# An encoder layer's expert stage: tiles of 96 slots of one expert and 32 of another group's, one accumulating scatter each

## The reference, cut to what matters

```python
g_idx = top_k(softmax(h @ w_rg + b_rg), 1)                  # one group of 4
e_idx = top_k(softmax(le of that group), 2)                 # two experts in it
a = einsum('bsd,edf->bsef', h, w_gate)                      # 1024 -> 256 per expert
u = einsum('bsd,edf->bsef', h, w_up)
hid = silu(a) * u * combine[..., None]
x = x + einsum('bsef,efd->bsd', hid, w_down)                # 256 -> 1024
```

## Time and profile before

| | us |
|---|---|
| median of 3 runs | 559.99 (556.28 to 560.72) |
| profiled execution, its own time | 559.87 |
| its span | 558.0 |
| mean granted TensorE clock | 0.930 of full speed |

### The profile page before, as it was taken

The page is one execution under the profiler, slowest core; times in us unless marked ns, Lnnn a source line. Parts: engine busy times, 40 slices in busy tenths (PEclk is TensorE's granted clock), DMA queues, the critical chain, the costliest instruction groups (busy, mean ns, idle before and its releaser), DMA issues. The chain is left out here.

```text
span 558.0 us, 7597 instructions
## 1 busy us (share of the span) xinstructions
PE 499.4 (89%) x2858; PEld 267.9 (48%) x2858; DVE 230.0 (41%) x642; ACT 113.8 (20%) x273; POOL 165.6 (30%) x167
## 2 busy tenths in 40 slices
PE   5898899998998999999999997854999999999970
PEld 3554444444664777665666666553333333333320
DVE  1127444412678834444545555452522322223110
ACT  2200242223232243332222311130011000110010
POOL 1211288850789700000000002221035222222242
PEclk9999799998998999999999977665999999999995
DMA  8999500005100000066000229386589999999712
GB/s 290 427 384 404 231 1 1 1 1 194 50 2 0 1 1 0 2 260 267 1 0 1 75 81 374 150 321 234 169 324 342 400 377 388 378 375 380 226 25 32
DMA packets 29609, 100.04 MB, mean 179 GB/s; under 512 B 5376, under 2 KB 6912, under 8 KB 29184
## 3 DMA queue, kind: packets, MB, share of 16 engines
q1 hardware_dynamic: 21216, 84.03, 39.1%
q0 software_dynamic: 5904, 8.43, 6.3%
q10 hardware_dynamic: 2448, 7.04, 3.3%
HBM read 77.39 MB, written 35.21 MB: 202 GB/s over the span
## 5 line engine op out<-in xcount | busy, mean ns | idle before, releaser
L1217 PE MATMUL bank<-arena 128*128 128x512 f32 (+1 forms) x256 | 114.9, 587 | 5.5 <-DVE arena L826 3.1
L1467 PE MATMUL bank<-arena 128*32 128x512 f32 x832 | 93.1, 599 | 0.0
L1192 PE MATMUL bank<-arena 128*128 128x128 f32 (+1 forms) x412 | 61.9, 287 | 21.0 <-DVE arena L908 4.6
L1217 PEld LDWEIGHTS bank<-arena 128*128 128x128 f32 x256 | 49.6, 196 | 61.4 <-issue 54.7
L1192 PEld LDWEIGHTS bank<-arena 128*128 128x128 f32 (+1 forms) x412 | 50.9, 145 | 57.9 <-issue 44.6
L585 POOL DMA_INDIRECT out<-arena x25 | 38.7, 1549 | 122.6 <-DVE arena L1143 49.6
L1355 PE MATMUL bank<-arena 128*128 128x512 f32 x128 | 65.0, 637 | 0.0
L1467 PEld LDWEIGHTS bank<-arena 128*32 128x32 f32 x832 | 25.8, 111 | 57.9 <-issue 57.9
L908 DVE COPY arena<-bank 128x512 f32<-128x512 f32 (+2 forms) x64 | 36.4, 587 | 36.4 <-PE bank L1192 36.3
L467 POOL TENSOR_SCALAR small<-small 128x1 f32<-128x1 f32 x16 | 3.7, 233 | 157.6 <-ACT arena L680 97.1
L1487 PE MATMUL bank<-arena 128*32 128x512 f32 x416 | 47.0, 592 | 0.8 <-DVE arena L1136 0.8
(11 more groups left out here) (153 smaller groups left out, 517.0 us busy)
## 6 DMA issues: line engine op xcount, KB each, us to landing
arena<-in_w_gu SPq DMA_DIRECT2D x17, 2048.0 KB
arena<-in_w_dn SPq DMA_DIRECT2D x17, 1024.0 KB, 20.6
slot_rows<-arena SPq DMA_DIRECT2D x1, 11308.0 KB, 37.8
arena<-slot_rows ACTq DMA_DIRECT2D x13, 514.0 KB, 6.7
arena<-in_w_out SPq DMA_DIRECT2D x2, 2048.0 KB, 8.0
arena<-in_x SPq DMA_DIRECT2D x4, 512.0 KB, 10.7
arena<-in_w_in_k SPq DMA_DIRECT2D x1, 2048.0 KB, 16.3
arena<-in_w_in_q SPq DMA_DIRECT2D x1, 2048.0 KB, 22.3
```

The lines of the kernel that those rows point to most:

```text
L1192: last = nc.tensor.transpose(TPB[p % 2][0:s.shape[-1], b * P:(b + 1) * P], s, ident)
L1217: last = nc.tensor.matmul(product_bank(i)[:, 0:width], hT[:, k, t * P:(t + 1) * P], w[:, k, :], start=(k == 0), stop=(k == KD - 1))
L1467: last = nc.tensor.matmul(GU[g % 2][BLK * b:BLK * (b + 1), :], xT[g % 2][:, k, BLK * b:BLK * (b + 1)], w_gu[n % RING][:, k, :], start=(k = ...
```

## The change

A tile is now made of two pieces. `TRIPLES` lists, for each group of tiles i, the first three experts of group i and the last expert of group i+2 (modulo 4): [0, 1, 2, 11], [4, 5, 6, 15], [8, 9, 10, 3], [12, 13, 14, 7]. Tile 3i+j holds the 96 slots of the j-th expert and, behind them, slots 32j to 32j+31 of the fourth one. The slots in DRAM stay where they were, so `load_x` needs two DMAs. As the two experts of a tile are of different groups, no token stands in it twice, and one scatter serves the tile; each waits for the one before to land. The weights are loaded in the order `LOADED`, and the table `BUF` says into which buffer each load goes (that whose last tile comes first).

```diff
+TRIPLES = [[EPG * i + j for j in range(3)] + [EPG * ((i + 2) % G) + 3] for i in range(G)]
+LOADED = [TRIPLES[i][j] for i in range(G) for j in (0, 3, 1, 2)]
+def last_tile(n):
+    i, j = divmod(n, 4)
+    return 3 * i + (0, 2, 1, 2)[j] if n < E else ITEMS + n - E
+def buffers():
+    buf, use, before = [], [], []
+    for n in range(E + EXTRA):
+        held = {b: max(m for m in range(n) if buf[m] == b) for b in set(buf)}
+        b = n if n < RING else min(held, key=lambda b: (last_tile(held[b]), held[b]))
...
+            i, j = divmod(g, 3)
+            return 3 * [4 * i + (0, 2, 3)[j]] + [4 * i + 1] if g < ITEMS else 4 * [E + g - ITEMS]
+        def rows_of(g):
+            if g >= ITEMS:
+                return x_dram[g * P:g * P + CAP, :], x_dram[g * P + CAP:(g + 1) * P, :]
+            i, j = divmod(g, 3)
+            own, shared = CAP * TRIPLES[i][j], CAP * TRIPLES[i][3] + BLK * j
+            return x_dram[own:own + CAP, :], x_dram[shared:shared + BLK, :]
+        def adds(g):
+            return 16 * (g // 3 + 1)
...
-            def add(g, run):
+            def add(g):
                 pool.wait_ge(s_ya, g + 1)
                 pool.wait_ge(s_yv, g + 1)
                 pool.wait_ge(s_tag, g + 1)
+                if g > 0:
+                    pool.wait_ge(s_add[(g - 1) % 3], adds(g - 1))
                 nc.gpsimd.indirect_dma_start(
-                    out=out_rows, out_offset=bass.IndirectOffsetOnAxis(ap=tag_row[:, g, run:run + 1], axis=0),
+                    out=out_rows, out_offset=bass.IndirectOffsetOnAxis(ap=tag_row[:, g, 0:1], axis=0),
...
+            for g in range(LAST + 1):
+                add(g)
+                if g < 2:
+                    overflow(2 * g)
+                    overflow(2 * g + 1)
...
-                nc.scalar.dma_start(xg[g % 3], x_dram[g * P:(g + 1) * P, :]).then_inc(s_xg[g % 3], 16)
+                for part, src in ((slice(0, CAP), rows_of(g)[0]), (slice(CAP, P), rows_of(g)[1])):
+                    nc.scalar.dma_start(xg[g % 3][part, :], src).then_inc(s_xg[g % 3], 16)
...
-                nc.vector.tensor_tensor(tag_row[:, g, :], row[:, R_TOK:R_TOK + 1].to_broadcast([P, 2]), cut, ALU.add)
+                nc.vector.tensor_scalar(tag_row[:, g, :], row[:, R_TOK:R_TOK + 1], float(FAR), None, ALU.add)
```

More of the change, by code:

```diff
@@ L49 @@
 RING = 5
+TRIPLES = [[EPG * i + j for j in range(3)] + [EPG * ((i + 2) % G) + 3] for i in range(G)]
[8 more added lines that the diff above has]
+        b = n if n < RING else min(held, key=lambda b: (last_tile(held[b]), held[b]))
+        before.append(held.get(b))
+        buf.append(b)
+        use.append(buf.count(b))
+    return buf, use, before
+BUF, USE, BEFORE = buffers()
 K_TRI, K_ONE, K_E, K_BASE, K_I = 0, P, 2 * P, 2 * P + E, 2 * P + 2 * E
 K_ROW = K_I + EXTRA
-K_CUT = K_ROW + T
-K_MINE = K_CUT + 2 * ITEMS + 1
+K_MINE = K_ROW + T
 NK = K_MINE + ITEMS
@@ L387, in expert @@
                 if n < E:
-                    return n
+                    return LOADED[n]
                 sp.wait_ge(s_extra, 1)
@@ L584, in add @@
                 pool.wait_ge(s_tag, g + 1)
+                if g > 0:
+                    pool.wait_ge(s_add[(g - 1) % 3], adds(g - 1))
                 nc.gpsimd.indirect_dma_start(
-                    out=out_rows, out_offset=bass.IndirectOffsetOnAxis(ap=tag_row[:, g, run:run + 1], axis=0),
+                    out=out_rows, out_offset=bass.IndirectOffsetOnAxis(ap=tag_row[:, g, 0:1], axis=0),
                     in_=y_sb[g % 3], in_offset=None,
                     bounds_check=SEQ - 1, oob_is_err=False, compute_op=ALU.add).then_inc(s_add[g % 3], 16)
[L590 to L613, removed]
+            for g in range(LAST + 1):
[3 more added lines that the diff above has]
+                    overflow(2 * g + 1)
             def extra_pool(g):
-                added(g - 1, 0)
-                add(g, 0)
-                added(g, 0)
+                add(g)
+                pool.wait_ge(s_add[g % 3], adds(g))
             passes(pool, extra_pool)
@@ L1467, in gate_up @@
                         last = nc.tensor.matmul(GU[g % 2][BLK * b:BLK * (b + 1), :], xT[g % 2][:, k, BLK * b:BLK * (b + 1)],
-                                                w_gu[n % RING][:, k, :], start=(k == 0), stop=(k == KD - 1))
+                                                w_gu[BUF[n]][:, k, :], start=(k == 0), stop=(k == KD - 1))
                 last.then_inc(s_gu, 1)
@@ L1488, in down @@
                                                     hidT[g % 2][:, k, BLK * b:BLK * (b + 1)],
-                                                    w_dn[n % RING][:, k, half * 512:(half + 1) * 512],
+                                                    w_dn[BUF[n]][:, k, half * 512:(half + 1) * 512],
                                                     start=(k == 0), stop=(k == 1))
@@ L1557 @@
         np.tile(CAP * p[:E], (P, 1)), np.tile(p[:EXTRA], (P, 1)), p[:, None] + P * p[:T] - FAR,
-        FAR + FAR * np.stack([p[:, None] >= cut, p[:, None] < cut], axis=2).reshape(P, 2 * ITEMS),
-        np.full((P, 1), FAR), (P * p[:ITEMS] + p[:, None]) // CAP], axis=1).astype(f32)
+        *[np.where(p < CAP, t[j], t[3])[:, None] for t in TRIPLES for j in range(3)]], axis=1).astype(f32)
     def by_expert(v, blocks):
```

50 lines of the change are left out of this document (24 added, 26 removed).

## The result

The kernel before took 557.81 us (median of 20 runs, 552.2 to 561.57), the changed one 565.25 us (20 runs, 559.81 to 571.27). The ratio is 1.0135, interval 1.0101 to 1.0168: **slower by 1.35%**, outside the predicted range of 552.4 to 557.8. How long its waits are in the other executions, no trace shows.

What follows compares the result with a forecast made beforehand. PE was taken to bound the expert stage, except at its start and tail. From 559.9 us, -5.0 (tail) and +0.3 (start) sum to -4.7, giving 555.2 us; range 552.4 to 557.8.

Steps and rivals of the forecast that it cites:

- The tail: End of the expert stage: with one scatter for tile 11, the last tile's scatter is issued 5.0 us earlier.
- B: Rival, tail: tile 11's scatter lands within 4.1 us, so the last tile's own data binds; 553.6 us, chance 0.05.
- two loads for a tile's rows: Row loads on ACT: the second DMA costs zero in mid-stage and +0.3 us at the stage's start.
- Weights ... Zero: Weight loads 5 to 16: each issued when it was, tightest slack 4.5 us at tile 10, so zero cost.
- The size of the start: Stage start: the second row piece delays PE's first tile by +0.3 us, bounds 0 to 0.7.
- Rival A: Stage start: the 32-row piece lands only after a further transfer, at most 3 us more; 558.2 us, chance 0.10.
- Rival C: Tile 10: split loads and bunched scatters make weights late; 10 us later would give 560.6 us; chance 0.03.
- Scatters before the tail, tags, buffers: Expert stage: twelve fewer scatters on POOL, changed tag adds on DVE and other weight buffers each change the time by zero.

Runs made afterwards that it cites:

- e3: Kernel before with one scatter for each tile in place of two runs, to substitute target rows; 548.77 us, ratio 0.9897 to before.
- e7: Changed kernel with before's row load, one DMA of 128 consecutive slots, filled slots as before, substitute target rows; 550.52 us, ratio 0.9898 to before.
- e1: Kernel before with only each row load split in two, over 96 and 32 partitions; 563.88 us, ratio 1.0148 to before.
- e8: Kernel before with each row load split into two halves of 64 partitions; 567.51 us, ratio 1.0193 to before.
- e2: Kernel before with each row load split by columns into two DMAs, each over all 128 partitions; 557.02 us, ratio 1.0028 to before.
- e4: Changed kernel with slots in DRAM in tile order, so one 128-partition DMA loads a tile's rows; 554.74 us, ratio 0.9997 to before.
- e6: The kernel of e4 with weights loaded in plain expert order, so most slots get wrong weights; 556.71 us, ratio 1.0008 to before.
- e10: The kernel of e4 with the substitute scatter target rows of e3; 555.15 us, ratio 1.0009 to before.
- e9: The kernel of e4 with odd tiles turned, so filled slots alternate between the halves from tile to tile; 554.13 us, ratio 0.9936 to before.
- e5: The kernel of e4 with an expert's second and third block of 32 slots exchanged; 556.5 us, ratio 0.9964 to before.

## Why the prediction was wrong

**The tail was right**, the mechanism and the size. Predicted -5.0, measured -5.1 in the profiled executions. Tile 11's 61 rows landed in 5.84 us (5.7 taken), the next scatter followed 0.85 us behind (0.77 taken). It stayed the bound by its predecessor's landing, so B did not happen. e3 and e7, which have this part without the split loads, are 1% faster.

**The step that failed** is the part on two loads for a tile's rows, and with it "Weights ... Zero". I costed the second load by its issue on ACT (0.34 us, hidden) and by its bytes (unchanged), and took the 16 engines' time for those bytes as fixed. It isn't. Loads over 96 and 32 partitions stretch the packets of q1 that run beside them, from 0.156 to 0.203 us, and thus take the slack from weights that they have nothing to do with. e1 shows it alone (1.0148 where nothing else changed), e8 with another shape (1.0193), and e2 excludes the number of DMAs (1.0028).

That is one part of the loss. Split and merge alone would make 1.0148 x 0.9897 = 1.0044 (an estimate that takes them as independent); the changed kernel has 1.0135. The remaining 0.9% goes with where the filled slots lie in a tile, which the prediction did not consider. e4 against e7 puts it at 1.0% (0.9997, 0.9898). Both figures are hardly larger than their uncertainty; that the effect is there rests on the traces, as said below.

At the one place where I weighed a rule, "DMA: Bandwidth & Descriptors" of the Trainium skill (Rules for kernel authors), its advice for one 128-partition transfer was right, and its reason, that two pieces serialize on the same engines, led me to price only a fixed cost. The rule that I left out is on another page of the Trainium skill, "SBUF — State Buffer" (Door 1: The DMA port swizzle): a transfer's bandwidth depends on how many of 16 ports its partitions reach, and partitions 0 to 63 reach 8 of them. The runs agree in their order, 128 partitions 0.151 to 0.156 us a packet, 96 and 32 0.20 to 0.21, 64 and 64 0.226. That ports are the cause, no run here shows; nor does that section speak of transfers of other queues, which is what cost the time here.

**The size of the start.** +0.3 predicted, with 0.7 as its bound; from issue to gate_up it was +2.1, and +0.9 more since gate_up began at a lower clock than in the earlier trace rows. Rival A had priced a later second piece at up to 3 us more, at 0.10; e2 puts 0.9 of the 2.1 on the doubled number of DMAs and leaves the other 1.2 to the shape.

**Rival C, at 0.03, was what came.** Its place was wrong, tile 10 for tiles 7 and 9, and its price too: I left out that a wait can cost PE its clock, so that 7.8 us of waits made 13.4. (C's own sums are off by 0.1: 4.5 + 4.7 = 9.2 us to use up the gain, and 560.7 us for 10 us; nothing hangs on it.) Place and slack were wrong for one reason: I took a load as landed when only the bytes behind it are left on q1. By that count load 14 had the least slack, 4.5 us, and load 13 7.3. In the changed kernel load 13 lands some 8.5 us later than by the count (505.5 against 497.0). The count can't say how far apart the engines are. The reports can, and they were in the trace of before: load 13's last came at 488.6, 3.7 us ahead of its use at 492.33, and load 14's at 502.0, 2.0 us ahead of 504.01 where the prediction had 4.5.

**Scatters before the tail, tags, buffers:** zero is borne out by e3 and e7, in which PE never waits for weights. It holds with the placement of filled slots in those two. In the changed kernel's own placement PE loses 2.4, 2.8 and 3.8 us even with whole row loads (e4, e6, e10), in e9's 0.5. That the placement matters is shown by e4 and e9, which differ in it and in the few numbers that compute it: 2.7 MB gone ahead in the one, 1.4 in the other. The ratios alone would not carry this, as their intervals overlap; the traces do.

*How* it does: the 16 reports of load 13 say more than the bytes. The page "DMA: Bandwidth & Descriptors" of the Trainium skill (The descriptor swizzle) gives, for a plain 128-partition transfer, partitions 0 to 63 to eight of the engines and 64 to 127 to the other eight. Were a scatter's rows dealt out by that section's rule (an estimate), the filled slots of tiles 0 to 6, whose scatters stand ahead of load 13's landing, would give the engines the rows in the third column. A scattered row takes about 0.33 us of an engine: from 475.5 to 480 us the changed kernel's q0 moves 0.32 MB, 78 rows, in 35.8% of 16 engines' time.

| placement | traces | rows, least and most busy engine | difference x 0.33 us | reports of load 13, first to last |
|---|---|---|---|---|
| turned | e9 | 28, 44 | 5.3 us | 6.0 us |
| before | e2, e7, e3, e1 | 28, 48 | 6.6 us | 5.4, 6.3, 6.8, 7.0 us |
| spread | e5 | 28, 50 | 7.3 us | 9.5 us |
| tile order | e4, e6, e10, changed | 20, 56 | 11.9 us | 13.4, 13.6, 14.3, 15.4 us |

The groups fit as well. In tile order the estimate has eight engines with 20 to 30 rows, five with 40 to 50 and three with 56; in the changed kernel eight reports come from 490.0 to 495.9 us, five from 498.9 to 501.7, three from 504.9 to 505.4. In e5 it has three engines with 48 to 50 rows and none else above 38; thirteen reports come from 485.4 to 489.0 us, three from 492.6 to 494.9. All this speaks for scatter rows, dealt out unevenly, as what sets the engines apart. It is not proof: the trace does not say which engine a report is from, and e8 has before's placement and yet 9.2 us, so uneven rows are not the only thing that spreads the reports.

Open as well: why a load over fewer partitions slows its neighbours. Other counts of partitions, or such a load beside a stream of weights and nothing else, were not tried.

## What to carry to other kernels

A DMA's cost to others is neither its issue time nor its bytes: before splitting a load by partitions, look at the rate of the stream beside it, and rather change the layout in DRAM so that one load still covers all 128 partitions (e4 against the changed kernel: from 1.0135 to 0.9997). Slack worked out from a queue's remaining bytes is an upper bound, since a load lands with its slowest engine (4.5 us by the count, 2.0 by the reports); count the filled rows that each part of the partitions gets; and price a long wait of PE with the slower clock that may stand behind it. Two good parts can hide in one bad change: the merge alone was worth 1% (e3), and e9, with whole loads and another placement, keeps 0.64% of it.

## What the runs showed of the hardware

- Row loads over 96 and 32, or 64 and 64, partitions raise the time of another queue's 4 KB packets from 0.156 us to 0.20 to 0.21, or 0.226, and lower the rate of all from 417 to 318 and 312, or 285 GB/s. The same bytes in two column halves over 128 partitions leave it at 0.151 us and 414 GB/s.
- After PE idled 3.8 and 4.0 us, its granted clock was half for 5 to 6 us of its work, and 64 matmuls took 9.60 and 9.97 us instead of 7.07. After waits of 0.42 to 1.68 us they took 7.07 to 7.08. In between it went either way: 8.77 us after 2.74 (e1), 7.07 after 2.86 (e10). After 5.64 us (e8) the 32 matmuls of down took 5.86 us instead of 3.64.
- An accumulating scatter of 61 rows of 4 KB landed 5.84 us after its issue, one of 34 rows in 4.73 us.
- An accumulated row of 4 KB takes about 0.33 us of an engine, a plain 4 KB packet 0.151 to 0.156.
- The 16 reports of one 2 MB load come over 5.4 to 7.0 us with the filled slots as before, over 13.4 to 15.4 us in tile order.
- A load of weights landed when up to 2.7 MB queued behind it had already moved (e4), 1.4 MB with the filled slots in other places (e9), with the same bytes in both.
